# Joints between a residual's last products and the next layer: order of evictions and sums, centring of the second half, and the sixth products

## The reference

```
x = layer_norm(ALPHA * x + mixer(x))           # layer 0: gated DeltaNet, layer 1: short convolution
x = layer_norm(ALPHA * x + conv_ffn(x))        # up (1024 -> 5632), convolution, gate, down (2816 -> 1024)
x = x + (p[i] @ w_proj[i]) * sigmoid(x @ w_gate[i])      # p[i] has 256 features
layer_norm: mu = mean(x); var = mean((x - mu)^2); (x - mu) * rsqrt(var + eps) * g + b
```

## Time and profile before

| | |
|---|---|
| median of 3 runs | 1806.93 us |
| profiled execution | 1807.6 us, span 1805.8 us |
| PE busy | 1745.5 us, 97% of the span |
| DVE, ACT, POOL busy | 1131.7, 457.5, 286.0 us |
| mean granted clock of PE | 0.993 |

### The profile page before, as it was taken

One profiled execution on the slowest core, in us unless ns is written; L12 is line 12 of the kernel. 1 busy time (PEld: TensorE's weight loads), 2 busy tenths in 40 slices (PEclk: granted clock), 3 DMA queues, 4 the chain that ended last, 5 costly groups with the idle time before them and its releaser, 6 DMA issues. The chain is left out here.

```text
span 1805.8 us, 21924 instructions
## 1 busy us (share of the span) xinstructions
PE 1745.5 (97%) x7699; PEld 1358.2 (75%) x7699; DVE 1131.7 (63%) x2177; ACT 457.5 (25%) x1092; POOL 286.0 (16%) x582
## 2 busy tenths in 40 slices
PE   8999999998899999999999999989899999999999
PEld 5677789985667777777776777766677777777767
DVE  4756787859776766773337655557776676643365
ACT  2433406633232222220004101112322222200041
POOL 0111106545320000000112000003200000001120
PEclk9999999999999999999999999999999999999999
DMA  4232210024112222242130222211122222331211
GB/s 148 71 110 83 78 59 13 1 106 152 47 48 82 82 71 82 82 141 84 65 106 24 94 70 81 84 57 47 47 71 83 82 71 82 124 106 71 94 37 53
DMA packets 45340, 139.36 MB, mean 77 GB/s; under 512 B 4896, under 2 KB 12192, under 8 KB 45232
## 3 DMA queue, kind: packets, MB, share of 16 engines
q1 hardware_dynamic: 41504, 132.90, 22.4%
q10 hardware_dynamic: 3728, 5.07, 0.9%
HBM read 129.63 MB, written 8.31 MB: 76 GB/s over the span
## 5 line engine op out<-in xcount | busy, mean ns | idle before, releaser
L269 PE MATMUL bank<-z,ring 128*128 128x288 f32 x1952 | 509.8, 408 | 8.4 <-DVE z L367 3.4
L269 PEld LDWEIGHTS bank<-z,ring 128*128 128x128 f32 x1952 | 372.0, 191 | 115.6 <-issue 3.5
L269 PE MATMUL bank<-x,ring 128*128 128x288 f32 x1632 | 431.0, 412 | 10.1 <-DMA x<-in_x 6.2
L269 PEld LDWEIGHTS bank<-x,ring 128*128 128x128 f32 x1632 | 313.3, 193 | 102.8 <-issue 13.6
L1994 DVE SCALAR_TENSOR_TENSOR scratch<-scratch 128x592 f32<-128x592 f32 x176 | 146.3, 832 | 25.5 <-ACT scratch L1938 23.9
L269 PE MATMUL bank<-y,ring 128*128 128x288 f32 x616 | 156.8, 406 | 3.0 <-DVE x L1776 2.0
L269 PEld LDWEIGHTS bank<-y,ring 128*128 128x128 f32 x616 | 116.8, 190 | 36.3 <-issue 2.4
L269 PE MATMUL bank<-big,ring 128*128 128x288 f32 x536 | 136.6, 410 | 6.8 <-issue 5.3
L269 PEld LDWEIGHTS bank<-big,ring 128*128 128x128 f32 x536 | 102.5, 192 | 36.8 <-issue 8.6
L2028 POOL COPY scratch<-scratch 128x2 f32<-128x2 f32 x88 | 26.0, 295 | 462.5 <-ACT scratch L1924 462.5
L1938 ACT ACTIVATE scratch<-scratch 128x592 f32<-128x592 f32 x88 | 69.4, 789 | 91.0 <-DVE scratch L1968 89.6
(11 more groups left out here) (358 smaller groups left out, 2407.8 us busy)
## 6 DMA issues: line engine op xcount, KB each, us to landing
ring<-in_w_up SPq DMA_DIRECT2D x88, 512.0 KB, 3.5
ring<-in_w_qkv SPq DMA_DIRECT2D x24, 512.0 KB, 3.5
ring<-in_w_scin SPq DMA_DIRECT2D x24, 512.0 KB, 3.5
ring<-in_w_down SPq DMA_DIRECT2D x12, 704.0 KB, 4.1
scratch<-in_w_down SPq DMA_DIRECT2D x12, 704.0 KB, 4.9
ring<-in_w_z SPq DMA_DIRECT2D x8, 512.0 KB, 3.5
big<-in_st_S SPq DMA_DIRECT2D x16, 256.0 KB, 5.2
out_dn_S_sample<-big SPq DMA_DIRECT2D x16, 256.0 KB, 2.6
```

Source lines behind the costliest of these rows:

```text
L269: last = pe.matmul(bank[:, 0:HALF], w[:, k * P:(k + 1) * P], rhs(k), start=start and k == 0, stop=k == self.depth - 1, skip_group_check=no ...
```

## The change

1. `sums` of half 1 takes the last piece (n = 15) itself: POOL no longer adds it to `sum_y` and DVE no longer adds its square; PE accumulates two more matmuls by the matrix of ones, from the piece and from its square in SQ. The counts become 15 and 13 per layer norm instead of 16 and 14.
2. The evictions of DVE come ahead of the sums: in joints 2 and 4, c12(3) after the first four scalings; in joints 1 and 3, c12(2) and c12(3) before most of the weight sums of the next layer, of which `sum2` and `sum3` of pair 1 move into the second half.
3. Half 0's inverse deviation comes from ACT: `Ln`, then `Exp` with scale -0.5; DVE's reciprocal goes there. Half 1 keeps square root and reciprocal; a one-column `Sqrt` (`root_table`) is issued behind half 0's affines.
4. Half 1 is centred by POOL alone, all 8 tiles.
5. In `up_act` and `ple_act` the `deviation` of half 1 comes before `copy_s1(1)`.
6. In both `up` layers p6(0) and p6(1) become one loop over k with both pairs in each step.
7. `project` takes banks 0, 1, 2 and 4 for its first four; ACT copies two of them out among half 0's affines, and four of the others among half 1's; p6 no longer waits for the last two.
8. DVE in `ple` makes all weight sums of pairs 0 and 1 before the second half; in the second half `token3`/`token2` of a tile come before the next two scalings.

```
 class Residual:  # nth_square(n): 13 * number + (13 if n == 15 else its place); add_square for n < 15 only
 def sums(self, pe, half):
-    pe.wait_ge(y_added, 16 * L + last + 1)
+    pe.wait_ge(y_added, 15 * L + last + 1)      # last: now the last n below 15 of this half
     ...
+    pe.matmul(BANK[6][:, 0:HALF], ONES[:], sum_y[:, cols], start=True, stop=not half)
+    if half:
+        r.made(pe, end)
+        pe.matmul(BANK[6][:, 0:HALF], ONES[:], r.piece(r.place[end][1], half), start=False, stop=True)
+    pe.wait_ge(sq_added, 13 * L + r.adds.index(last) + 1)
+    last = pe.matmul(BANK[7][:, 0:HALF], ONES[:], sum_sq[:, cols], start=True, stop=not half)
+    if half:
+        pe.wait_ge(squared, 16 * (L + 1))
+        last = pe.matmul(BANK[7][:, 0:HALF], ONES[:], SQ[r.nth_square(end) % 2], start=False, stop=True)
+    last.then_inc(ln_sums, 1)
 def deviation(self, act, half):
+    if half: act.activation(rs, rs, ACT.Sqrt, bias=eps_ln).then_inc(ln_std, 1)
+    else:
+        act.activation(rs, rs, ACT.Ln, bias=eps_ln).then_inc(ln_std, 1)
+        act.wait_ge(ln_std, at + 1)
+        act.activation(rs, rs, ACT.Exp, scale=-0.5).then_inc(ln_inverse, 1)
+def root_table(self, act): act.activation(CV[:, 154:155], eps_ln, ACT.Sqrt)
+def p6_both(self, pe):
+    ...
+    for k in range(self.depth):
+        pe.wait_ge(token2_made, self.token_base + k + 1)
+        for i in range(2):
+            last = self.run(pe, BANK[2 + (self.base + i) % 2], i, "s2", self.t(2), True, None, (k,))
 class LayerNorm:
-    DVE_PIECES = 2
+    DVE_PIECES = (2, 0)
 class InputGate:
+    def bank(self, n): return (0, 1, 2, 4)[n] if n < 4 else 2 + n % 4
 def ple_pe(pe, layer):
     g.project(pe, slice(0, 4))
+    pe.wait_ge(projected_out, 2 * DT * layer + 2)
     ... g.project(pe, slice(4, None))
-        pe.wait_ge(projected_out, 2 * DT * (layer + 1))
+        pe.wait_ge(projected_out, 2 * DT * (layer + 1) - 2)
 def residual_act(act, r):   # behind the 8 affines of half 0
+    n.root_table(act)
     for x in range(13, 16): r.square(act, x)
 def down_act(act, layer):
     for m in range(DT):
         n.affine(act, 0, m)
-    r.square(act, 15)
+        if m == 3:
+            gate[layer].projection(act, slice(0, 2))
+            r.square(act, 15)
+    n.root_table(act)
 def ple_act(act, layer):
-    g.projection(act, slice(0, 4)); g.copy_s1(act, 0); n.mean(act, 1); g.copy_s1(act, 1); n.deviation(act, 1)
+    g.projection(act, slice(2, 4)); g.copy_s1(act, 0); n.mean(act, 1); n.deviation(act, 1); g.copy_s1(act, 1)
+    for j, m in enumerate(n.ORDER[1]):
+        n.affine(act, 1, m)
+        if j >= 4: g.projection(act, slice(j, j + 1))
+    g.projection(act, slice(8, None))
 def down_dve(dve, layer):   # the end
     n.variance(dve, 0)
-    r.add_square(dve, 14); n.centre_dve(dve, 0); n.inverse(dve, 0); n.scale(dve, 0, slice(0, None))
-    r.c12(dve, 3); r.add_square(dve, 15)
+    n.centre_dve(dve, 0); n.scale(dve, 0, slice(0, 4)); r.c12(dve, 3); r.add_square(dve, 14)
+    n.scale(dve, 0, slice(4, None))
 def end_residual_dve(dve, r, next_dense):   # the end
     r.add_square(dve, 12)
-    next_dense.sums123(dve, 0); r.c12(dve, 2); r.add_square(dve, 13); r.add_square(dve, 14)
-    next_dense.sum1(dve, 1); r.c12(dve, 3); r.add_square(dve, 15); next_dense.sum2(dve, 1); next_dense.sum3(dve, 1)
+    r.c12(dve, 2); next_dense.sum1(dve, 0); r.add_square(dve, 13); r.c12(dve, 3); r.add_square(dve, 14)
+    next_dense.sum2(dve, 0); next_dense.sum3(dve, 0); next_dense.sum1(dve, 1)
 def second_half_dve(dve, n, d, between):   # between(0): sum2(1), between(1): sum3(1), in up layers alone
     n.variance(dve, 1)
-    n.centre_dve(dve, 1)
+    between(0)
     n.inverse(dve, 1); n.scale(dve, 1, slice(0, 4))
     for k in range(KH):
-        if k < 2: n.scale(dve, 1, slice(4 + 2 * k, 6 + 2 * k))
         dve.wait_ge(ln_ready, n.nth(1, KH + k)); d.token3(dve, k); d.token2(dve, k)
+        if k < 2: n.scale(dve, 1, slice(4 + 2 * k, 6 + 2 * k))
+    between(1)
 # POOL: add_piece(15) goes in all joints; centre_pool(1, slice(2, 8)) becomes slice(0, 8) in all four
```

More of the change, by code:

```diff
@@ L1730, in square @@
                 else:
-                    at = 14 * self.number + self.adds.index(n)
+                    at = self.nth_square(n)
                     if at >= 2:
@@ L1824, in sums @@
                 order = self.residual.order
-                last = max(n for n in range(2 * DT) if self.residual.place[n][0] == half)
-                pe.wait_ge(y_added, 16 * L + last + 1)
+                r, end = self.residual, 2 * DT - 1
+                last = max(n for n in range(end) if r.place[n][0] == half)
+                pe.wait_ge(y_added, 15 * L + last + 1)
                 if 2 * L + half:
@@ L1842, in deviation, with root_table @@
                 act.wait_ge(ln_var, 2 * at + 2)
-                act.activation(rs[:, cols], rs[:, cols], ACT.Sqrt, bias=eps_ln).then_inc(ln_std, 1)
+                if half:
+                    act.activation(rs[:, cols], rs[:, cols], ACT.Sqrt, bias=eps_ln).then_inc(ln_std, 1)
+                else:
+                    act.activation(rs[:, cols], rs[:, cols], ACT.Ln, bias=eps_ln).then_inc(ln_std, 1)
+                    act.wait_ge(ln_std, at + 1)
+                    act.activation(rs[:, cols], rs[:, cols], ACT.Exp, scale=-0.5).then_inc(ln_inverse, 1)
+            def root_table(self, act):
+                act.activation(CV[:, 154:155], eps_ln, ACT.Sqrt)
             def affine(self, act, half, m):
@@ L1867, in centre_dve @@
                 dve.wait_ge(ln_mean, 2 * at + 2)
-                for m in self.ORDER[half][:self.DVE_PIECES]:
+                for m in self.ORDER[half][:self.DVE_PIECES[half]]:
                     y = self.residual.piece(m, half)
@@ L2057, in projection @@
                     act.wait_ge(projected, 2 * DT * self.layer + n + 1)
-                    act.activation(self.out[:, m, half * HALF:(half + 1) * HALF], BANK[2 + n % 4][:, 0:HALF], ACT.Copy
+                    act.activation(self.out[:, m, half * HALF:(half + 1) * HALF], BANK[self.bank(n)][:, 0:HALF], ACT.Copy
                                    ).then_inc(projected_out, 1)
@@ L2348, in steady_start @@
             d.p2(pe, 1)
-            d.p6(pe, 0)
-            d.p6(pe, 1)
+            if sums:
+                d.p6_both(pe)
+            else:
+                d.p6(pe, 0)
+                d.p6(pe, 1)
             d.p7(pe, 0)
@@ L2560, in up_dve, with second_sums @@
             f, d = ffn[layer], up[layer]
-            second_half_dve(dve, norm[2 * layer], d)
+            def second_sums(step):
+                if step == 0:
+                    d.sum2(dve, 1)
+                else:
+                    d.sum3(dve, 1)
+            second_half_dve(dve, norm[2 * layer], d, second_sums)
             f.u1(dve, 0)
@@ L2678, in down_dve @@
             n.variance(dve, 0)
+            n.centre_dve(dve, 0)
+            n.scale(dve, 0, slice(0, 4))
+            r.c12(dve, 3)
             r.add_square(dve, 14)
-            n.centre_dve(dve, 0)
-            n.inverse(dve, 0)
-            n.scale(dve, 0, slice(0, None))
-            r.c12(dve, 3)
-            r.add_square(dve, 15)
+            n.scale(dve, 0, slice(4, None))
         def end_residual_dve(dve, r, next_dense):
@@ L2736, in end_residual_dve, with second_half_dve @@
             r.add_square(dve, 12)
-            next_dense.sums123(dve, 0)
             r.c12(dve, 2)
+            next_dense.sum1(dve, 0)
             r.add_square(dve, 13)
+            r.c12(dve, 3)
             r.add_square(dve, 14)
+            next_dense.sum2(dve, 0)
+            next_dense.sum3(dve, 0)
             next_dense.sum1(dve, 1)
-            r.c12(dve, 3)
-            r.add_square(dve, 15)
-            next_dense.sum2(dve, 1)
-            next_dense.sum3(dve, 1)
-        def second_half_dve(dve, n, d):
+        def second_half_dve(dve, n, d, between=lambda step: None):
             n.variance(dve, 1)
-            n.centre_dve(dve, 1)
+            between(0)
             n.inverse(dve, 1)
@@ L2900, in mixer_pool @@
             n.centre_pool(pool, 0, slice(5, 8))
-            for x in range(12, 16):
+            for x in range(12, 15):
                 r.add_piece(pool, x)
```

65 lines of the change are left out of this document (38 added, 27 removed).

## The result

The changed kernel takes 1790.91 us (median of 4 runs, 1788.62 to 1792.27), the kernel before on the same chip 1807.58 (4 runs): ratio 0.9906, interval 0.9889 to 0.9923, so 16.7 us or 0.9% faster. The forecast was 1787.8 with a range of 1783.5 to 1796. The profiled execution took 1790.41 us, 17.2 less than the 1807.6 from which the sum was made; the sum said 19.5.

What follows compares the result with a forecast made beforehand. PE, busy 97% of the span, was taken as the bound, losing 43 us at four joints. Savings of 4.55 + 0.6 + 3.7 + 0.9 + 4.9 + 4.9 = 19.5 us gave 1787.8 us, range 1783.5 to 1796.

Steps and rivals of the forecast that it cites:

- the main case: Whole kernel: the summed savings come as worked out, 1787.8 us, own range 1785.5 to 1790.5; chance 0.64.
- the clock rival: Joints 1 and 3: longer idle before p6 brings half clock outlasting the tokens, 3.6 us less gain, 1791.7; chance 0.16.
- Joint 1, up to p1(0): Half 0's inverse by Ln and Exp starts DVE's scalings earlier; p1(0) at 488.2, not 490.40: 2.2 us saved.
- Joint 1, the sums: PE waits 0.45 within four sum matmuls, ACT reads at 492.55; saved up to here 4.55 us, in joint 3 3.7.
- The slower rival: Sums wait for square 15 behind ACT's list and DVE's add_squares; decides from some 5 us delay, 1815; chance 0.04.
- Half 1 up to p7: Joints 1 and 3, from the start of half 1's mean (T): p6 at T + 9.3; net 0.6 and 0.9 saved.
- I take 0.8: Joints 1 and 3, p6: cost of half clock lasting beyond the last token, 0.8 us each, up to 1.9 possible.
- The rival without loss: Half 1: DVE's scalings lose nothing beside POOL, 2 x 2.3 us more saved and no fallen clock, 1783; chance 0.07.
- The rival of dear tables: ACT's table switches cost twice 1.28 us each, 3 us less saved per joint, 1800; chance 0.04.
- Joints 2 and 4: Waits before project(3) and p6 go, 0.9 stays at late copies; p6 at 978.6, not 983.49: 4.9 us saved each.

Runs made afterwards that it cites:

- the filled idle: Changed kernel plus twelve matmuls with unread results in PE's idle before p6 in both up joints (1 and 3): 1787.76 us.
- with POOL alone: Changed kernel with last piece by POOL and DVE, Ln/Exp for half 1, and table load, copy_s1(1) and weight sums moved; POOL still centres all 8 tiles: 1786.94 us.
- the run of both together: Changed kernel with last piece by POOL and DVE, table load moved, Ln/Exp for half 1 too, and DVE centring three of its tiles: 1787.35 us.

## Why the prediction was right, and by how much it was off

Its mechanism came as said in each joint; two sizes were off, and they make most of the 2.3 us between 19.5 and 17.2: joint 1 fell short by 1.6, joint 3 by 0.45, joints 2 and 4 by 0.2 together. The median of 1790.91 lies in the stated range but just outside the 1785.5 to 1790.5 given for the main case, and nearer to the clock rival's 1791.7; it was not the clock that took it there, though, as the clock cost 1.8 us over both joints (below) where 1.6 was counted. By its own working (1788.1 less 0.7) the sum gives 1787.4, not the 1787.8 that was said.

- *Joint 1, up to p1(0)*: "**2.2 us** saved" was 1.35. p5(3) came as worked out, p3(2) 0.3 later. Then p3(3) was taken to follow p3(2) after 2.35 us (486.25), so with a wait of 0.4 at most; it followed after 2.86, because it waited for c22(3), which stands in DVE's order behind two scalings and two add_squares (to 486.5, with 0.1 us of idle among them). Before, it was the same 2.86:
```profile
488.38 2.18 PE L269 MATMUL bank<-big 128*128 128x288 f32 x8 [0.69 <-DVE x L1797]
```
No part of the change touches that stretch of DVE's list, and the working itself counted a loss there for the kernel before. That is the mis-sized term, together 0.8 us in each `up` joint; the run with c22(3) moved up, where p3(3) does not wait, bears it out.
- *Joint 1, the sums*: "waits 0.45 within them" was no wait at all: because p1(0) came 0.85 later, the last piece and its square were there. T was 493.13, not 492.55: 4.0 saved, not 4.55; in joint 3 3.1, not 3.7. c12(3) was done at 491.28 (490.83 + 0.45), not 490.85: the ladder of squares was 0.4 late as well, and it is luck that PE, later still, did not meet it. The slower rival decided from 5 us of delay there and had 0.4.
- *Half 1 up to p7*: p6 at T + 9.34 (9.3), tokens 1.6 apart, last at T + 13.3, idle 3.56 (3.6). The clock's price was the second term: "I take 0.8" was 1.4 in joint 1 and 0.4 in joint 3, by the filled idle. Together with p7 at 14.8 rather than 14.6 this half gained -0.3 and +1.1, not 0.6 and 0.9. The clock rival was thus half there: in joint 1 it came, in joint 3 not. The working's reason, that half clock costs nothing while tokens are late, was wrong: it set a step's 0.97 us at full clock against the 1.6 between tokens, where at half clock it is 1.94. That the two joints' errors nearly cancel is luck.
- *POOL and DVE*: the four scalings took 3.48 beside POOL and 1.60 without it (part 4 undone), against 3.3 and 1.6 in the working. The rival without loss is refuted. The Trainium skill (SBUF — State Buffer, Who interferes with whom, the single rule) calls the port pair that DVE and GpSimd share an exclusive lock, and this trace agrees in that both engines slow down together (1.04 and 1.00 us in place of 0.45 and 0.79). But undoing part 4 did not give the 2 us more a joint that the prediction drew from it: in the `up` joints the toll on the scalings was about what the earlier reciprocal had gained, and only the gates lost by part 4 (0.42 each).
- *Tables*: each switch cost 1.28 with the next ACTIVATE right behind (476.69 + 1.28, `Exp` at 477.98). The rival of dear tables is refuted. By the Trainium skill (ScalarE: Activation LUTs, Table sets: the hidden batching unit) `Ln` followed by `Exp` needs one load, as a set has both; the trace shows two. In joints 1 and 3 DVE was not free sooner, as the prediction said, so the second load cost nothing. In joints 2 and 4 DVE's first scaling waited 0.66 for `Exp` (948.25 in the rows of joint 2); whether any of that reached PE through ACT's late copies no run shows.
- *Joints 2 and 4*: 4.8 each for 4.9, with each of the three waits as worked out. Parts 7 and 8 were not undone by themselves: what they give is read from these traces only.

What each part was worth, where an experiment undid it: part 6 between 0.6 and 2.2 us (the lower with a like half clock), part 3 2.7 in the `up` joints (less 0.35 in the gates), part 4 costs 0.5, from single runs. Part 1 was undone only together with a moved table load; the two together gained 0.7 up to T in each `up` joint and nothing in the gates. If these add up, which was not tried, the rest, 13 to 15 of the 17 us, is that of parts 1, 2, 5, 7 and 8, which no run took apart: which of them did what is read from the waits that went, and argued, not shown.

## What to carry to other kernels

When a wait is for the last link of a long chain on three engines, try to reorder the chain before making links of it new work for the bounding engine: here two extra matmuls took 0.97 us at each joint, while POOL's addition, with the evictions ahead and the table load out of its way, left only 0.26 of the wait. When a wait is shortened, look for what stands behind the same instruction on the helping engine: the copy behind `Exp`, c22(3) behind the add_squares. And price an idle of the matmul engine by its length and by a half clock that may follow, and work out a step's time at half clock before calling it hidden. The length of the idle alone did not say whether the clock would fall; where an idle can't be removed, useless matmuls in it gave 1.8 and 1.5 us here over the two `up` joints.

## What was not expected of the hardware

- Most idles of 2.1 to 3.8 us of PE at the joints were followed by stretches of clock 0.50 of either 3.4 or 6.8 us, both lengths in one kernel at two joints with the same idle of 3.56; at 1190 us too it was one in some kernels and the other in others. Two such idles were not: 2.50 in joint 3 of the kernel before (clock 1.00 from 1262 to 1268) and 3.12 in joint 1 with POOL alone. Idles of 1.9 (p2(1), in the run of both together) were followed by half clock in two joints of four. Filled with 2 to 3 us of useless matmuls, the granted clock stayed 1.00, in two kernels at both joints; why it fell at some idles and not at others is open.
- DVE and POOL, each with 288-column operations of two inputs in SBUF, went on in step, one pair per 0.97 us, 1.04 for DVE in place of 0.45 and 1.00 for POOL in place of 0.79; a 512-column sum took 1.28 beside POOL in place of 0.68. The reciprocal took 1.94 wholly beside POOL (496.00 in after) and 1.94 where POOL worked only in its first 0.7 us (952.74 before); evictions from PSUM took 0.45 either way.
